# Later second modulation of the halo rows, and the last Q/K finishing inside the convolution's first tile, in a decoder-layer kernel on eight cores

## The reference, cut to what matters

```python
h = modulate(rms_norm(x, norm_ffn1), sh1, sc1)
x = x + 0.5 * gt1[:, None, :] * swiglu(h, ffn1_w_gate, ffn1_w_up, ffn1_w_down)
h = modulate(rms_norm(x, norm_mix), sh2, sc2)          # "second modulation"
x = x + gt2[:, None, :] * hybrid_mixer(h, ...)
h = modulate(rms_norm(x, norm_ffn2), sh3, sc3)
x = x + 0.5 * gt3[:, None, :] * swiglu(h, ffn2_w_gate, ffn2_w_up, ffn2_w_down)

# in hybrid_mixer
proj = h @ w_in                 # q | k | v (3 groups x 4 heads x 128) | u | B | C | gates
q = rms_norm(q, q_norm); k = rms_norm(k, k_norm)       # per head
xc = c_gate * u
conv = xp[:, 0:S] * conv_w[0]   # xp: xc padded by two rows on the left
for j in range(1, CONV_K):
    conv = conv + xp[:, j:j + S] * conv_w[j]
y_conv = (b_gate * conv) @ w_conv_branch
```

## Time and profile before

| what | value |
|---|---|
| median of 3 runs | 2338.02 us (2337.32 to 2342.23) |
| the profiled execution | 2341.5 us |
| its span (slowest core, core 1) | 2340.0 us |
| spans of the cores | 2325.1 to 2340.0 us |
| TensorE busy | 2249.8 us, 96% of the span |
| VectorE, ScalarE, GpSimd busy | 1086.1, 609.3, 503.6 us |
| mean granted TensorE clock, core 1 | 0.991 |

### The profile page before, as it was taken

The page is one execution under the profiler, slowest core; times in us unless marked ns, Lnnn a source line. Parts: engine busy times, 40 slices in busy tenths (PEclk is TensorE's granted clock), DMA queues, the critical chain, the costliest instruction groups (busy, mean ns, idle before and its releaser), DMA issues.

```text
span 2340.0 us, 32158 instructions; the slowest of 8 cores (2325.1 to 2340.0 us)
## 1 busy us (share of the span) xinstructions
PE 2249.8 (96%) x11524; PEld 1044.9 (45%) x11524; DVE 1086.1 (46%) x1846; ACT 609.3 (26%) x1045; POOL 503.6 (22%) x610
## 2 busy tenths in 40 slices
PE   2899999998999999999999999999999999999999
PEld 1444444443444444444544544444444444434444
DVE  1254543446534454464545444766433444454444
ACT  2501011133111111245676675211122111111110
POOL 2120211034211120133544545310011221010100
PEclk8999999999999999999999999999999999999999
DMA  9654644048465473468244426841111543141302
GB/s 178 133 68 50 80 65 54 1 112 212 64 81 64 52 104 80 86 154 73 33 48 47 56 33 85 110 48 25 48 48 52 101 78 39 14 70 26 55 37 108
DMA packets 255114, 168.20 MB, mean 72 GB/s; under 512 B 171760, under 2 KB 235376, under 8 KB 253040
## 3 DMA queue, kind: packets, MB, share of 16 engines
q0 software_dynamic: 146832, 129.52, 36.3%
q1 hardware_dynamic: 108128, 36.62, 8.3%
HBM read 208.98 MB, written 20.97 MB: 98 GB/s over the span
## 4 chain that ended last, share of the span: by engine, by line
PE 87%; DMA 4%; DVE 2%; ACT 2%; issue 2%; SPq 1%; POOL 1%; another core or an unknown queue 0%; DVEq 0%; ACTq 0%; POOLq 0%
PE ps L215 87%; DMA Dw<-ffn_w_gate 2%; DMA C<-C 1%; SPq L215 1%; DVE A L215 1%; ACT Dw L215 1%; ACT C L215 1%; DVE B L215 1%; POOL C L215 0%; ACT A L215 0%; DMA A<-Dw 0%; DVE E L215 0%; POOL rstd L215 0%; DMA B<-Dw 0%; DVE C L215 0%
## 5 line engine op out<-in xcount | busy, mean ns | idle before, releaser
L215 PE MATMUL ps<-B,Dw 128*128 128x512 bf16 x6144 | 1380.4, 381 | 33.1 <-DVE E L215 9.1
L215 PEld LDWEIGHTS ps<-B,Dw 128*128 128x128 bf16 x6144 | 595.6, 98 | 741.7 <-issue 61.4
L215 DVE TENSOR_TENSOR A<-ps,A 128x512 f32<-128x512 f32 (+2 forms) x764 | 478.7, 644 | 180.4 <-PE ps L215 174.0
L215 ACT ACTIVATE E<-ps 128x512 f32<-128x512 f32 x296 | 176.5, 596 | 1315.0 <-PE ps L215 1287.6
L215 DVE TENSOR_TENSOR E<-ps,E 128x512 bf16<-128x512 f32 (+1 forms) x288 | 198.8, 690 | 645.3 <-PE ps L215 627.2
L215 PE MATMUL ps<-Dw,E 128*128 128x512 bf16 x2048 | 463.6, 379 | 7.0 <-DVE A L215 5.9
L215 PEld LDWEIGHTS ps<-Dw,E 128*128 128x128 bf16 x2048 | 195.4, 98 | 258.9 <-issue 32.8
L215 ACT ACTIVATE Dw<-ps 128x512 bf16<-128x512 f32 (+2 forms) x280 | 163.3, 588 | 260.7 <-PE ps L215 252.9
L215 POOL DMA_DIRECT2D Dw<-ffn_w_gate x62 | 44.4, 717 | 492.1 <-PE ps L215 492.1
L215 PE MATMUL ps<-B,C 128*128 128x512 bf16 x512 | 121.0, 379 | 0.0
L215 POOL TENSOR_TENSOR Dw<-Dw 128x256 bf16<-128x256 bf16 (+1 forms) x128 | 101.2, 795 | 58.8 <-ACT Dw L215 44.7
(11 more groups left out here) (94 smaller groups left out, 1098.9 us busy)
## 6 DMA issues: line engine op xcount, KB each, us to landing
Dw<-w_in POOLq DMA_DIRECT2D x60, 256.0 KB, 6.7
Dw<-ffn_w_down POOLq DMA_DIRECT2D x58, 256.0 KB, 6.6
Dw<-ffn_w_gate POOLq DMA_DIRECT2D x48, 256.0 KB, 5.2
Dw<-ffn_w_up POOLq DMA_DIRECT2D x48, 256.0 KB, 5.4
C<-w_ada POOLq DMA_DIRECT2D x24, 512.0 KB, 9.4
A<-xo POOLq DMA_DIRECT2D x4, 2048.0 KB, 11.9
x1s<-A POOLq DMA_DIRECT2D x4, 2048.0 KB, 7.3
A<-x1s POOLq DMA_DIRECT2D x4, 2048.0 KB, 9.1
```

The source lines that it names most:

```text
L215: ins = getattr(engine, name)(*a, **kw)
```

## The change

Three edits. (1) The settle time of the halo rows' norm goes from 15.0 to 26.0: the eight modulations and the store behind them are recorded some 12 later by `P.t`. (2) The two flushes ahead of the convolution go; they run after the C and after the u product of the convolution's first tile, which takes banks 1 and 0 for itself (the counter `pctr` is a multiple of 3 there), and the last attention is put in its lane after that tile. (3) The halo tokens' product takes bank 3, not bank 2.

```diff
-            n2[0, tg] = Norm("n2", 1.5, tg, xn_a, 1, 16, 24, mid, put, hss[tg % 2], False, 15.0, before)
+            n2[0, tg] = Norm("n2", 1.5, tg, xn_a, 1, 16, 24, mid, put, hss[tg % 2], False, 26.0, before)
...
-    flush()
-    flush()
-    for a in ready:
-        a()
...
-            for w, pb in ((wc_, 2 + i2), (wu_, i2)):
+            pu, pc = (0, 1 + pctr[0] % 3) if fins else (i2, 2 + i2)
+            for w, pb in ((wc_, pc), (wu_, pu)):
                 for k in range(KC):
                     mm(pss[pb][:], w[:, k, :], hT[:, k, tk], k == 0, k == KC - 1)
-                if pb >= 2:
+                if fins:
+                    flush()
+                if w is wc_:
                     act(out=ctmp[i2], in_=pss[pb][:], func=AF.Copy)
                     if fc >= 1:
                         conv_taps(fc - 1, tb)
                 L.tick()
-            tt(out=xc[:, 4 * tb:4 * tb + 4, 1:129], in0=pss[i2][:].rearrange("p (n q) -> p n q", n=4),
+            if fins:
+                fins[:] = []
+                for a in ready:
+                    a()
+            tt(out=xc[:, 4 * tb:4 * tb + 4, 1:129], in0=pss[pu][:].rearrange("p (n q) -> p n q", n=4),
                in1=ctmp[i2].rearrange("p (n q) -> p n q", n=4), op=ALU.mult)
         for w, c in ((wu_, 0), (wc_, 2)):
             for k in range(KC):
-                mm(pss[2 + cctr[0] % 2][:, c:c + 2], w[:, k, :], h2t[:, k, :], k == 0, k == KC - 1)
-        ph = pss[2 + cctr[0] % 2]
+                mm(pss[3 - cctr[0] % 2][:, c:c + 2], w[:, k, :], h2t[:, k, :], k == 0, k == KC - 1)
+        ph = pss[3 - cctr[0] % 2]
```

## The result

The changed kernel took 2349.57 us, median of 10 runs (2342.81 to 2704.17); the kernel before, on the same chip, 2342.35 us (10 runs). The ratio is 1.003, with a 95% interval of 1.0021 to 1.004: slower by 0.3%, some 7 us on the slowest core. The forecast was 1.5 us faster, inside the band of no change.

What follows compares the result with a forecast made beforehand. The prediction took TensorE, busy 96% of the span, as the bound. Terms of +1.8, -3.1 and -0.25 summed to about -1.5 us from the 2338.0 us median: 2336.5 us, with an 8 in 10 range of 2331.5 to 2341.5.

Steps and rivals of the forecast that it cites:

- edit 1's term: First SwiGLU, later modulations and store: 0 us gained, 1.8 us added by the last stop; +1.8 us, bounds -4.4 and +5.
- Edit 3's term: Convolution's second block finds bank 2 free, but TensorE mostly waits later instead: -0.25 us, bounds 0 and -1.24.
- The 3.47 us: TensorE's longest wait in the first SwiGLU for a hidden block queued behind halo modulations; claimed to move, not go.
- Three stops cost about nothing, the fourth stays: `down` stops of 1.8 us per tile: the first three absorbed by waits for B, the last tile's 1.8 us remaining.
- The queue runs empty at the same 530: GpSimd's queue carries the same 3 MB without a break, ending at 530, so B transposes land when they did.
- B before 533: Sign against the forecast: B modulations of tile 0 in the first SwiGLU beginning before 533; forecast was 534 to 536.
- both terms: Convolution's start without the flushes: 1.5 us less idling, and 1.6 us from the clock staying up; together -3.1 us.
- The wait of 1.24 us: TensorE's idling at 1462.93 before the convolution's second block, claimed to go since the C product finds bank 2 free.
- 0.73 + 1.0 us of waits: TensorE's 0.73 us wait at 1481.31, before bank 4 in the convolution, claimed to become about 1.7.
- Slower: Rival, chance 0.07: modulations under GpSimd's scaling stop TensorE 4 us in each tile's `down`; +5.8 in all, 2343.8 us.
- The edit does what it says: Rival, chance 0.13: in the first SwiGLU transposes land 3.5 us sooner and modulations fit into `down`; -9.6, 2328.4 us.

## Why the prediction was wrong

**The step that failed** is edit 1's term: +1.8 us forecast; measured +5.8 on the halo stretch of the changed kernel, and +5.7 +-1.1 on the mean core span with edit 1 alone. It went wrong in who pays for the stops, in the fixed end of GpSimd's queue, and in leaving out what happens to the load that starts there. Edit 3's term had the wrong sign.

**What was right.** The 3.47 us moved to a wait for B and did not go. Stops in `down` came by the mechanism that was walked through, with modulations of 1.0 to 1.1 us beside the scalings: forecast 1.3 to 2.4 us in every group, measured 0.25 to 2.08 in 25 of 32. Seven ran without a stop, which the prediction had named as a sign against it.

**"Three stops cost about nothing, the fourth stays"** came near in its sum by luck. On the six cores without a stretched load the halo stretch grew by 2.3 us (137.1 to 139.4), against the +1.8 of the forecast. But the four stops are 4.5 us there in the mean, and TensorE's other waits fell from 8.3 to 6.0 only. The first and the third stop stayed nearly whole: the other waits of halo tile 3 went from 5.0 to 4.6 us, since B came later on most cores, and those of own tile 0 from 0.9 to 1.1. It was the fourth that found a wait to hide in: own tile 1 had 2.3 us of other waits before and has 0.3.

**The load.** The sum had no term for what happens to the load that starts beside VectorE's instructions. On cores 0 and 6 such a load was stretched, and the mean of eight rose by another 3.4 us. The time is that of the slowest core, though, so a thing that hits a core in 18 of 64 profiles hits at least one of eight in more than nine executions of ten (an estimate: 1 - (46/64)^8 = 0.93, if cores were independent). Core 0, with 17.17 us of waiting, was the slowest core. How much it adds varies: the same kernel measured again had four stretched loads in its profile and a ratio of 1.0011. I had bounded the edit at +5 by the largest stops; the rows of before held nothing to bound this with, as no load there was stretched. I priced what the moved instructions do to the engines that they now overlap, and not what they may do to the transfer that starts there. The runs that add VectorE's work to the kernel before show, however, that stretched loads aren't all: with one in eight the loss is 4.5 us of mean core span, and with none (the load on SP's queue) the halo stretch is still 3.5 us longer.

**"The queue runs empty at the same 530"** failed in both directions. The same 3 MB were in the queue, but the store now came when the load was nearly through, and moved beside the transposes. It landed between 526 and 537 us over the cores, and B of tile 0 began between 530.40 and 540.14 (before: 529.98 to 535.54). I had read from the earlier trace rows who waits for whom, and taken the end for fixed. "B before 533" was named as a sign against the forecast, and core 1, whose row it was, shows it. It gained by it: waits of 9.7 us between 500 and 612 us, where there had been 10.5, with four stops of 6.6 us among them. Why the store took 8.4 us on core 1 and 14.5 on core 3 isn't shown; SP's queue got 4048 packets through on core 1 between 523 and 531 us, and 1537 on core 3.

**Edit 2** was right in both terms. From the end of the last halo k to the first product it took 1.68 us and not 3.10: 1.4 us gained, forecast 1.5. The clock stayed up on every core: 1.6 us, as forecast. On core 6 of the kernel before it had stayed up too (1.00 from 1434 to 1442 us; a convolution stretch of 46.9 against 48.4 to 48.6 us), which bears the term out.

**Edit 3** was mis-sized, with the wrong sign. The wait of 1.24 us went; instead of 0.73 + 1.0 us of waits behind it there were 1.46 + 0.53 + 0.68 = 2.67. From the first halo product of the convolution to the second, TensorE took 19.74 us against 18.88 (19.56 to 19.74 on the eight cores against 18.85 to 18.89). VectorE is the bound there, as I had read in the earlier trace rows, but I took its own time for given. It wasn't. The timelines of DVE and of POOL on core 1 of the changed kernel, and then of DVE on core 1 of the kernel before:

```profile
1451.37 4.72 DVE L215 SCALAR_TENSOR_TENSOR C<-E,cw_s,C 128x640 f32<-128x640 f32 x4
```

```profile
1452.37 4.24 POOL L215 TENSOR_TENSOR Dw<-Dw 128x512 bf16<-128x512 bf16 x4 [0.59 <-ACT Dw L215]
```

```profile
1463.82 2.81 DVE L215 SCALAR_TENSOR_TENSOR C<-E,cw_s,C 128x640 f32<-128x640 f32 x4
```

The four taps that took 2.81 us, while GpSimd was done at 1464.2 and idle until 1466.2, now lie beside its products for their whole length and take 4.72. That the products are the cause wasn't tried by itself, and edits 2 and 3 were not run apart; but GpSimd's products before the first halo product begin 4.9 us ahead of it in both kernels, and the next ones 5.1 us behind it before and 3.7 after. Edits 2 and 3 together: -3.35 forecast, 2.0 measured on the stretch, 2.0 and 1.4 on the mean core span.

**The sum.** On these two stretches, in the mean of the cores, +2.4 + 3.4 - 2.0 = +3.8 us in place of -1.5; on the slowest core +7 (the 2.4 is the growth on the six cores over the mean of all eight before). The rival *Slower* had stops of 4 us and no absorption; that isn't what happened. *The edit does what it says* fell too: with the modulations out of VectorE's way (on ScalarE, edit 1 alone) the halo stretch is 1 us shorter, not 6.

## What to carry to other kernels

Before work is moved to where an engine has time, look at what else starts there: a short instruction on VectorE costs through GpSimd's operation beside it, through the additions queued behind it, and perhaps through the transfer that begins under it. Adding the same instructions to the unchanged kernel, on each engine in question, is a cheap way to price the place without moving anything. Where the slowest of eight cores counts, an event that is rare on one core is a cost of most executions, and the mean over the cores tells the parts of a change apart long before the slowest core does.

## What the runs showed of the hardware that I had not expected

- A load of 2 MB from GpSimd's queue can take 14.5 to 26 us in place of 8.4 to 13.2, with single 16 KB packets of 4 to 14 us; seen in 18 of 64 core profiles with VectorE's instructions at its start, only on the third and fourth of four such loads, in 2 of 64 without, in none of 8 on SP's queue.
- Both VectorE forms tried beside GpSimd's scaling cost the same (+4.5 and +4.7 us), the one-operand form and the product of two. ScalarE's eight beside the same scaling took 5.74 us in one run and 7.15 in another, and cost nothing.
- VectorE's f32 taps were slower as well where GpSimd multiplied beside them: four in 4.72 us against 2.81.
- A store of 1 MB that started beside the end of a load, with transposes waiting in SP's queue, took from 7.5 to 14.9 us on the cores of one execution (before, right behind the load's issue, 12.1 to 14.7). What decides it isn't shown.
